# Eight first projections as seven half-size products each, with their weight sums made by GpSimd and VectorE

## The chip, the cores and the metric

The kernel runs on one core of a Trainium2 chip. The metric is the device time of one execution in microseconds (us). Inside the core, TensorE multiplies matrices into eight PSUM banks, VectorE, ScalarE and GpSimd do elementwise work (GpSimd never on a bank), SyncE and GpSimd start transfers. They run their own instruction lists and meet only at semaphores.

## The reference

A two-layer block on 256 latent and 256 context tokens of width 1024, followed by a second two-layer block. The change touches the first layer's input projection of both token sets and what reads it:

```python
def even_layer_mixer(h, hc, w_in, w_out, lb, onorm_g, lam_p, subln_g, lambda_init, rope, need_ctx):
    p = h @ w_in
    pc = hc @ w_in
    ya, yac = hgrn2_mixer(p[..., :5 * A_WIDTH], pc[..., :5 * A_WIDTH], lb, onorm_g)
    yb, ybc = diff_attention_mixer(p[..., 5 * A_WIDTH:], pc[..., 5 * A_WIDTH:], lam_p, subln_g, lambda_init, rope, need_ctx)
    y = jnp.concatenate([ya, yb], axis=-1) @ w_out
...
def split(a):
    q, ff, fb, i, g = jnp.split(a, 5, axis=-1)
    q = heads(jax.nn.silu(q.astype(F32)) * (A_DK ** -0.5))
...
def gates(f_raw, lb_d):
    f = lb_d + (1.0 - lb_d) * jax.nn.sigmoid(f_raw.astype(F32))
    return 1.0 - f, jnp.log(f)
```

`w_in` is 1024 x 4096: eight pieces of 512 columns. Pieces 0 to 4 are q, the two gates, value and output gate of the gated recurrence; 5 to 7 are query, key and value of the differential attention. `h` is the normed input, scaled and shifted by vectors that a further matrix (`ada_w`) makes from a condition. After the two mixers come the output projection and a mixture of experts; nothing there is changed. All is float32.

## The kernel before

**Tiling.** Activations lie with features on the 128 partitions and 512 tokens (latent, then context) along the row: `H[:, k]` is feature tile k of 8. Weights come in chunks of 2 MB (1024 x 512) in the order of the list `CHUNKS` (line 88) into a ring of six slots (`SLOTS`); chunk n goes to slot n % 6. SyncE starts the loads in that order, each once TensorE has closed its last product on chunk n - 6 (`old_chunk_used`, line 1430). `("in1", 0, c)` is piece c of `w_in`, `("ada", l, c)` a modulation chunk.

**Banks.** TensorE's `open_job` takes the next bank of a cycle that `in_banks` sets, or a named one, and waits until the bank's last result was taken; `close_job` tells that it is filled. The readers call `result` (wait until filled) and count the bank as taken. `place_of` and `last_job` hold what stands where.

**Projections.** `project` (line 547) makes four output tiles of a chunk, each from 8 products of 128x128 weights with 512 token columns; `project_tokens` (563) does it with tokens as the output's partitions. One float32 matmul is two instructions in the profile. The order on TensorE is (lines 630 to 757):

1. chunk 5, then 6, each with a modulation chunk (`ada_main`, line 590; 16 instructions of 512 columns) behind each of its four tiles. VectorE turns the modulation sums (`modulation`, 2077), TensorE folds them (`ada_fold`, 607).
2. four products for the rope of q and k (line 641), which VectorE finishes (`rope`, 2112), and chunk 7.
3. the attention loop, 16 units (head, block of 128 queries) and two more rounds to drain it. Iteration i does the scores of unit i, half a tile of chunk 3 or 4 (`value_half`, `gate_half`), the transposes of unit i - 1 and the output of unit i - 2. VectorE finds the maxima (L2133), ScalarE the exponentials (L1704), VectorE scales and subtracts (L2141 to L2144).
4. squares and sums of the head norm (`head_sums`, 526) with chunk 0 in the middle, then chunks 1 and 2.
5. the diagonal scores of the recurrence ("hd", line 730), which wait for `hgrn_inputs`, three modulation chunks of the second layer, and seven levels of doubling in 14 steps (`STEPS`, line 741), with a modulation chunk in each of the first nine.

**Readers of the projections.** ScalarE copies chunks 5, 6, 3 and 4 out of the banks and takes the sigmoid of 0, 1 and 2 straight from them (L1726 to L1731); VectorE copies chunk 7 (L2126), multiplies q by its sigmoid (L2177) and turns the sigmoids into gates (L2183, L2184). Then it makes `A0` from the diagonals and two products over whole pages (L2195, L2197), for which the first level waits. GpSimd has nothing to do from its first three loads until chunk 2 is projected; then it makes one product per step of the levels (L1543), from and to SBUF like VectorE's of the same steps (L2211, L2220).

**Memory.** `pages` are 13 pieces of 2048 columns, reused by every stage; `extra` (3072 columns) holds ScalarE's copies for the levels.

## Time and profile before

| | us |
|---|---|
| three timed runs | 2184.03, 2185.76, 2185.82 (median 2185.76) |
| profiled execution, span from its first to its last instruction | 2180.4 |
| TensorE busy in it | 2032.8 |
| VectorE busy | 686.1 |
| ScalarE busy | 410.1 |
| GpSimd busy | 96.8 |

The profile gives the span of the profiled execution, not its whole time. An engine is busy while it executes; the instructions that only wait or start transfers do not count. The changed part lies between 44 and 346 us.

### The profile page before, as it was taken

The numbers are of one execution on the slowest core, as the hardware profiler recorded it, in microseconds if no ns is written. First come the engines' busy times: TensorE is split into PE (matmuls) and PEld (weight loads), VectorE is DVE, ScalarE is ACT, GpSimd is POOL, SyncE is SP. The second block draws the span as 40 slices with busy tenths as digits, with TensorE's granted clock in tenths as the row PEclk, the third lists the DMA queues.
The fourth block names the chain that finished last, engine by engine and source line by source line (L and its number), as shares of the span: only waits on it lengthen the run. The fifth ranks groups of instructions, "written<-read, shape, count | busy, mean of one in ns | idle before, by whom it ended". The sixth has DMA issues, their size and how long they took to land. (4 is left out here: it accounts for less than half of the span.)

```text
span 2180.4 us, 25566 instructions
## 1 busy us (share of the span) xinstructions
PE 2032.8 (93%) x10076; PEld 1077.9 (49%) x10076; DVE 686.1 (31%) x1583; ACT 410.1 (19%) x872; POOL 96.8 (4%) x92
## 2 busy tenths in 40 slices
PE   5999999896999999999799799999999899998999
PEld 2345546643334334333475533333333766577887
DVE  3034217525110110111547211111111698711411
ACT  2014302212110110111225211111111232421101
POOL 0000004201000000001000100000000000000000
PEclk9999999997999999999899899999999999798999
DMA  9761118412999999999731599999999723233240
GB/s 361 264 234 39 51 65 312 198 43 98 404 417 406 412 419 407 416 406 403 297 116 37 194 416 428 428 410 429 428 429 418 266 97 112 93 122 130 78 155 20
DMA packets 114655, 570.08 MB, mean 261 GB/s; under 512 B 6288, under 2 KB 20880, under 8 KB 89984
## 3 DMA queue, kind: packets, MB, share of 16 engines
q1 hardware_dynamic: 105440, 537.71, 62.0%
q0 software_dynamic: 6688, 25.65, 3.2%
q10 hardware_dynamic: 2432, 5.38, 0.6%
q8 instruction: 69, 1.13, 0.2%
q14 instruction: 26, 0.21, 0.0%
HBM read 560.20 MB, written 8.52 MB: 261 GB/s over the span
## 5 line engine op out<-in xcount | busy, mean ns | idle before, releaser
L556 PE MATMUL banks<-pages,weight_ring 128*128 128x256 f32 (+1 forms) x1984 | 520.5, 423 | 8.5 <-ACT pages L1676 3.2
L556 PEld LDWEIGHTS banks<-pages,weight_ring 128*128 128x128 f32 x1984 | 378.8, 192 | 149.1 <-issue 102.3
L1029 PE MATMUL banks<-weight_ring,pages 128*64 128x512 f32 x964 | 217.3, 597 | 4.3 <-DMA weight_ring<-in_moe_w_gate 1.5
L2004 DVE TENSOR_TENSOR pages<-banks,pages 128x512 f32<-128x512 f32 (+3 forms) x175 | 100.1, 612 | 366.0 <-PE banks L936 177.6
L1775 ACT ACTIVATE pages<-banks 128x512 f32<-128x512 f32 (+1 forms) x147 | 82.5, 572 | 675.8 <-PE banks L966 133.3
L966 PE MATMUL banks<-weight_ring,pages 128*64 128x512 f32 x896 | 198.6, 598 | 7.8 <-issue 3.1
L2004 DVE TENSOR_TENSOR pages<-pages 128x512 f32<-128x512 f32 (+7 forms) x267 | 166.5, 643 | 13.3 <-POOL pages L1543 3.7
L1651 ACT ACTIVATE pages<-banks 128x256 f32<-128x256 f32 (+2 forms) x196 | 81.4, 441 | 460.8 <-PE banks L556 339.2
L2004 DVE TENSOR_TENSOR pages<-pages,banks 128x512 f32<-128x512 f32 (+1 forms) x41 | 28.2, 688 | 401.4 <-PE banks L1029 175.5
L1029 PEld LDWEIGHTS banks<-weight_ring,pages 128*64 128x64 f32 x964 | 67.4, 137 | 147.4 <-issue 133.2
L966 PEld LDWEIGHTS banks<-weight_ring,pages 128*64 128x64 f32 x896 | 63.0, 138 | 135.9 <-issue 130.3
L1139 PE MATMUL banks<-weight_ring,pages 128*64 128x512 f32 x512 | 114.3, 596 | 6.0 <-DVE pages L2498 5.4
L1139 PEld LDWEIGHTS banks<-weight_ring,pages 128*64 128x64 f32 x512 | 35.0, 137 | 74.3 <-issue 61.7
L570 PE MATMUL banks<-weight_ring,pages 128*128 128x512 f32 (+1 forms) x192 | 70.3, 523 | 0.0
L770 PE MATMUL banks<-pages,weight_ring 128*128 128x512 f32 x128 | 57.2, 606 | 3.2 <-DVE pages L2245 3.2
L1006 PE MATMUL banks<-weight_ring,pages 128*128 128x512 f32 x128 | 55.9, 595 | 0.0
L1424 PE MATMUL banks<-weight_ring,pages 128*128 128x256 f32 x256 | 55.4, 379 | 0.0
L1093 PE MATMUL banks<-weight_ring,pages 128*64 128x512 f32 x224 | 51.2, 598 | 3.9 <-issue 3.9
L599 PE MATMUL banks<-weight_ring,small 128*32 128x512 f32 x384 | 47.3, 616 | 7.6 <-DMA weight_ring<-in_ada_w 6.7
L1057 PE MATMUL banks<-weight_ring,pages 128*64 128x512 f32 x224 | 50.1, 596 | 3.6 <-DVE pages L2498 1.9
L570 PEld LDWEIGHTS banks<-weight_ring,pages 128*128 128x128 f32 x192 | 36.1, 190 | 32.7 <-issue 31.1
L1424 PEld LDWEIGHTS banks<-weight_ring,pages 128*128 128x128 f32 x256 | 48.6, 190 | 6.6
(317 smaller groups left out, 1887.8 us busy)
## 6 DMA issues: line engine op xcount, KB each, us to landing
weight_ring<-in_moe_w_down SPq DMA_DIRECT2D x64, 2048.0 KB, 18.3
weight_ring<-in_moe_w_gate SPq DMA_DIRECT2D x62, 2048.0 KB, 17.7
weight_ring<-in_moe_w_up SPq DMA_DIRECT2D x62, 2048.0 KB, 19.4
weight_ring<-in_ada_w SPq DMA_DIRECT2D x24, 2048.0 KB, 16.3
weight_ring<-in_even_w_in SPq DMA_DIRECT2D x18, 2048.0 KB, 19.8
weight_ring<-in_odd_w_in SPq DMA_DIRECT2D x8, 2048.0 KB, 9.0
weight_ring<-in_odd_w_out SPq DMA_DIRECT2D x6, 2048.0 KB, 8.4
weight_ring<-in_odd_w_qkv SPq DMA_DIRECT2D x3, 2048.0 KB, 14.1
```

Source lines behind the costliest of these rows:

```text
L556: last = pe.matmul(b[:, 0:w], s[:, k, m * P:(m + 1) * P], src(k)[:, t0:t0 + w], start=(k == 0), stop=(k == nk - 1))
L570: last = pe.matmul(b[:, 0:n], src(k)[:, t * P:(t + 1) * P], s[:, k, c0:c0 + n], start=(k == 0), stop=(k == nk - 1))
L770: last = pe.matmul(at, s[:, k + 4 - 4 * half, m * P:(m + 1) * P], (yB, g1)[half][:, k], start=(half == 0 and k == 0), stop=(half == 1 and ...
L966: last = pe.matmul(b[n], xg[:, par, 4 * half + k, 0:64], w_[:, k, 512 * n:512 * n + 512], start=(half == 0 and k == 0), stop=(half == 1 an ...
L1006: last = pe.matmul(b, xg[:, par, 4 * half + k], w_[:, k, 512 * n:512 * n + 512], start=(half == 0 and k == 0), stop=(half == 1 and k == 3))
L1029: last = pe.matmul(to, xg[:, par, k, 64 * half:64 * half + 64], rows, start=(half == 0 and k == 0), stop=(half == 1 and k == 3))
L1093: last = pe.matmul(whole[64 * a:64 * a + 64], hidT[:, f, 64 * half:64 * half + 64], w_[:, f, 512 * a:512 * a + 512], start=(half == 0 and ...
L1139: last = pe.matmul(b[64 * a:64 * a + 64], hidT[:, f, 64 * half:64 * half + 64], w_[:, f, 512 * a:512 * a + 512], start=(half == 0 and f == ...
L1424: last = pe.matmul(b[:, 0:256], yp[:, k, t * P:(t + 1) * P], w_[:, k], start=(k == 0), stop=(k == 15))
L1651: act.activation(dst, b[:, 0:w], func).then_inc(taken_sem(job), 1)
L1775: act.activation(dst, banks_mem[:, use(l, job)[0], 0:n], func).then_inc(moe_taken(l, job, 0)[0], 1)
L2004: return dve.tensor_tensor(out_, a, b, op)
```

## The change

Each of the eight chunks is one level of a seven-product scheme for a product of 2 x 2 blocks. The weights of a chunk are cut into four blocks of 512 features x 256 columns, the tokens' side into four of 512 features x 256 tokens. TensorE makes seven products M1 to M7 of 512 x 256 by 512 x 256; four sums of weight blocks, four sums of token blocks and seven additions of results go with them. A product fills one bank and is 16 instructions of 256 columns.

The token sums T1 to T4 are made once by VectorE. The weight sums of chunks 5, 6 and 7 are made by VectorE, in pages; those of 3, 4, 0, 1 and 2 by GpSimd, in slots of the ring: five `("sum", 0, c)` entries stand in `CHUNKS`, for which nothing is loaded, and the chunks behind them move up by one to five places. ScalarE copies M1 out of its bank (`in1_first`); VectorE adds the other six in (`in1_out`), M5 with two instructions. The quarters of q and of the gates get their sigmoid by ScalarE from SBUF afterwards. In the loop, iteration i < 16 has a product: chunk 3 in iterations 0 to 6, chunk 4 in 7 to 13, the first two of chunk 0 in 14 and 15; its other five stand in the head norm. The three modulation chunks of the second layer move from behind the diagonal scores to in front of them. The temporary row of the head norm moves to another page.

```diff
-          + [("in1", 0, c) for c in (7, 3, 4, 0, 1, 2)]
+          + [("in1", 0, 7)]
+          + [(kind, 0, c) for c in (3, 4, 0, 1, 2) for kind in ("in1", "sum")]
...
+    PRODUCTS = {c: ("M1", "M6", "M2", "M7", "M5", "M4", "M3") for c in range(8)}
+    PRODUCTS[5] = ("M1", "M2", "M6", "M7", "M5", "M4", "M3")
+    PAIR = {5: (3, 4), 6: (5, 6), 7: (4, 5), 3: (6, 7), 4: (7, 6), 0: (6, 7), 1: (5, 0), 2: (7, 6)}
+    IN_FIRST = ("M1", "M2", "M5", "M3")
+    SUMMED = (5, 6, 7, 3, 4, 0, 1, 2)
+    IN1_TO = {5: qB, 6: kB, 7: vB, 3: v1, 4: g1, 0: q1, 1: ff, 2: fb}
+    token_side = [extra[:, 1024 * n:1024 * n + 1024].rearrange("p (k t) -> p k t", k=4) for n in range(3)]
+    TSUM = {"T1": token_side[0], "T2": token_side[1], "T3": H[:, 0:4, NX:NTOK], "T4": token_side[2]}
...
+    def sum_parts(w_, to):
+
+        a11, a12 = w_[:, 0:4, 0:NX], w_[:, 4:8, 0:NX]
+        a21, a22 = w_[:, 0:4, NX:512], w_[:, 4:8, NX:512]
+        return ((0, a21, a22, ALU.add), (2, a11, a21, ALU.subtract), (1, to[:, 0], a11, ALU.subtract),
+                (3, a12, to[:, 1], ALU.subtract))
...
+                "M1": (w_[:, low, 0:NX], H[:, low, 0:NX], 0, 0),
+                "M2": (w_[:, high, 0:NX], H[:, high, 0:NX], 0, 0),
+                "M3": (sums[:, 3], H[:, high, NX:NTOK], 4, 0),
+                "M4": (w_[:, high, NX:512], TSUM["T4"], 0, 8),
+                "M5": (sums[:, 0], TSUM["T1"], 1, 1),
+                "M6": (sums[:, 1], TSUM["T2"], 3, 3),
+                "M7": (sums[:, 2], TSUM["T3"], 2, 2)}[product]
...
+            job = in1_job(c, product)
+            b = open_job(job, PAIR[c][0 if product in IN_FIRST else 1])
+            still, moving = (token_side, weight_side) if c in TOKEN_ROWS else (weight_side, token_side)
+            for a in range(2):
+                for k in range(4):
+                    if c == 5 and a == 0 and product in ("M1", "M2"):
+                        pe.wait_ge(sem("norm_h"), 2 * (k + (4 if product == "M2" else 0)) + 1)
+                    last = pe.matmul(b[:, a * NX:(a + 1) * NX], still[:, k, a * P:(a + 1) * P], moving[:, k],
+                                     start=(k == 0), stop=(k == 3))
+            close_job(job, last)
...
-        project("m1", ("in1", 0, 5), h, KT, 4, NTOK, norm="norm_m1", per_k=2, after=ada_beside(4))
-        project("m1", ("in1", 0, 6), h, KT, 4, NTOK, after=ada_beside(8))
+        for c, first in ((5, 4), (6, 8)):
+            for n in range(7):
+                in1_product(c, n)
+                if n < 4:
+                    ada_main(0, first + n)
...
-            if i < 8:
-                value_half(i)
-            elif i < 16:
-                gate_half(i - 8)
+            if i < 16:
+                in1_product((3, 4, 0)[i // 7], i % 7)
...
-        in_banks(*range(8))
-        head_sums("dn", pages(8).rearrange("p (h t) -> p h t", h=4), pages(9, P, 1664),
-                  lambda: project("m1", ("in1", 0, 0), h, KT, 4, NTOK))
+        def rest_of_query():
+            for n in range(2, 7):
+                in1_product(0, n)
+
+        in_banks(*range(5))
+        head_sums("dn", pages(8).rearrange("p (h t) -> p h t", h=4), RS, rest_of_query)
         for c in (1, 2):
-            project("m1", ("in1", 0, c), h, KT, 4, NTOK)
-
+            for n in range(7):
+                in1_product(c, n)
+
+        in_banks(*range(7))
+        for c in range(3):
+            ada_main(1, c)
         pe.wait_ge(sem("diff_done"), 1)
         pe.wait_ge(sem("hgrn_inputs"), 1)
         for c in range(4):
@@ -735,9 +806,6 @@
                     last = pe.matmul(b[:, hd * P:(hd + 1) * P], kk[:, hd, c * P:(c + 1) * P],
                                      q1[:, hd, c * P:(c + 1) * P], start=(n == 0), stop=(n == 1))
             close_job(job, last)
...
-        in_banks(*range(7))
-        for c in range(3):
-            ada_main(1, c)
...
+        for c in BY_POOL:
+            wait_weights(pool, ("in1", 0, c))
+            filled_by_now(last_job[CHUNKS[NUMBER["sum", 0, c] - SLOTS]])
+            w_, to = slot(("in1", 0, c), KT, 512), sums_of(c)
+            for n, (dst, a, b, op) in enumerate(sum_parts(w_, to)):
+                if n >= 2:
+                    pool.wait_ge(sem("pool_sums"), first_sums(c) + (1 if n == 2 else 3))
+                pool.tensor_tensor(to[:, dst], a, b, op).then_inc(sem("pool_sums"), 1)
...
+        def weight_sums(c):
+
+            wait_weights(dve, ("in1", 0, c))
+            if c == 7:
+                result(dve, in1_job(5, "M3"))
+            w_, to = slot(("in1", 0, c), KT, 512), sums_of(c)
+            for n, (dst, a, b, op) in enumerate(sum_parts(w_, to)):
+                if n >= 2:
+                    dve.wait_ge(sem("sums"), first_sums(c) + (1 if n == 2 else 3))
+                tt(to[:, dst], a, b, op).then_inc(sem("sums"), 1)
...
+            if product in ("M6", "M2"):
+                wait_taken(dve, in1_job(c, "M1"))
+                dst, plus = (second if product == "M6" else quad(c, 0, 0)), first
+            elif product == "M7":
+                for done in ("M2", "M6"):
+                    wait_taken(dve, in1_job(c, done))
+                dst, plus = first, second
+            elif product == "M5":
+                wait_taken(dve, in1_job(c, "M7"))
+                tt(quad(c, 1, 1), b, first, ALU.add)
+                dst, plus = second, second
+            elif product == "M4":
+                dst, plus = quad(c, 1, 0), first
+            else:
+                wait_taken(dve, in1_job(c, "M5"))
+                dst, plus = quad(c, 0, 1), second
+            tt(dst, b, plus, ALU.add).then_inc(taken_sem(job), 1)
...
+        dve.wait_ge(sem("norm_h"), 16)
+        low, high = slice(0, 4), slice(4, 8)
+        token_sum("T1", H[:, low, NX:NTOK], H[:, low, 0:NX])
+        token_sum("T3", H[:, high, NX:NTOK], H[:, low, NX:NTOK])
+        dve.wait_ge(sem("sums"), 1)
+        token_sum("T2", H[:, high, NX:NTOK], TSUM["T1"])
+        weight_sums(5)
+        dve.wait_ge(sem("sums"), 3)
+        token_sum("T4", H[:, high, 0:NX], TSUM["T2"])
...
+        for c in (5, 6):
+            for product in PRODUCTS[c][1:5]:
+                in1_out(c, product)
+            weight_sums(c + 1)
+            for product in ("M4", "M3"):
+                in1_out(c, product)
         modulation(1, 0, 4, 8)
...
+        for product in ("M6", "M2", "M7", "M5"):
+            in1_out(7, product)
...
+                c, product = (3, 4, 0)[i // 7], PRODUCTS[0][i % 7]
+                if product != "M1":
+                    in1_out(c, product)
...
+            for product in ("M6", "M2", "M7", "M5"):
+                in1_out(1 + d, product)
+            for product in ("M4", "M3"):
+                in1_out(1 + d, product)
+            for m in (2, 3, 0, 1):
+                dve.wait_ge(sem("in1_sigmoid"), 4 + 4 * d + (3 if m >= 2 else 4))
...
```

## Rows read from the trace of the kernel before

**Rows 1.** The page: TensorE's busy time, and its granted clock in 40 slices (tenths).

```profile
PE 2032.8 (93%) x10076; PEld 1077.9 (49%) x10076; DVE 686.1 (31%) x1583; ACT 410.1 (19%) x872; POOL 96.8 (4%) x92
...
PEclk9999999997999999999899899999999999798999
```

**Rows 2.** Timeline, 40 to 151 us: start, us, engine, line, ..., [idle before, releaser].

```profile
43.07 6.49 ACT L1676 ACTIVATE pages<-pages,small 128x256 f32<-128x256 f32 x16 [2.75 <-DVE pages L2026]
...
44.12 9.72 PE L556 MATMUL banks<-pages,weight_ring 128*128 128x512 f32 x16 [1.60 <-ACT pages L1676]
...
53.77 1.93 PE L599 MATMUL banks<-weight_ring,small 128*32 128x512 f32 x16
...
55.63 7.13 PE L556 MATMUL banks<-pages,weight_ring 128*128 128x512 f32 x16
...
64.54 7.13 PE L556 MATMUL banks<-pages,weight_ring 128*128 128x512 f32 x16
...
119.03 0.33 PE L614 MATMUL banks<-pages,small 128*32 128x32 f32 x16 [0.90 <-DVE pages L2082]
...
122.86 27.63 PE L570 MATMUL banks<-weight_ring,pages 128*128 128x512 f32 x64
```

**Rows 3.** TensorE's timeline from chunks 1 and 2 to the first level.

```profile
274.59 55.17 PE L556 MATMUL banks<-pages,weight_ring 128*128 128x512 f32 x128 [1.85 <-DVE pages L2177]
...
331.70 9.01 PE L735 MATMUL banks<-pages 128*128 128x128 f32 x64 [1.94 <-issue]
...
346.20 2.89 PE L752 MATMUL banks<-pages,extra 128*128 128x128 f32 x16 [0.20 <-DVEq L2200]
```

**Rows 4.** Line 1424: ns min/median/max, first and last start (us), form.

```profile
L1424 PE MATMUL banks<-weight_ring,pages x256: 379/379/379, 2119.7 to 2174.7; 128*128 128x256 f32 x128
```

**Rows 5.** VectorE's timeline: the transposes, and the end of the ropes.

```profile
118.19 0.45 DVE L2081 STREAM_TRANSPOSE pages<-banks 128x256 f32<-128x256 f32 x1 [69.28 <-PE banks L599]
...
128.88 1.42 DVE L2004 TENSOR_TENSOR pages<-pages 128x512 f32<-128x512 f32 x2
```

**Rows 6.** VectorE's timeline in the levels, and GpSimd's products by line.

```profile
352.21 1.23 DVE L2004 TENSOR_TENSOR pages<-pages 128x1024 f32<-128x1024 f32 x1 [2.20 <-POOL pages L1543]
...
358.91 3.66 DVE L2004 TENSOR_TENSOR pages<-pages 128x1024 f32<-128x1024 f32 x1
...
362.49 1.40 DVE L2245 COPY_PREDICATED pages<-pages,banks 128x512 f32<-128x512 uint32 x2
...
L1543 POOL TENSOR_TENSOR pages<-pages x13: 1963/3151/3617, 349.2 to 397.1; 128x1024 f32<-128x1024 f32 x13
```

**Rows 7.** The ring's tile, 70 to 120 us: issue ns, first and last start.

```profile
L1444 SPq DMA_DIRECT2D weight_ring<-in_ada_w x4: 368/1976/5542, 80.6 to 85.1; - x4
...
DMA to landing us min/median/max: 7.9/18.7/21.7
```

**Rows 8.** Windows: last three columns are granted clock, DMA share, GB/s.

```profile
87.00:90.00 3.00, 3.00 (x14) 1.02 (x16) 0.00 (x0) 0.45 (x1) 0.00 (x0) 1.00 1.05 388
...
334.00:336.00 2.00, 2.00 (x11) 2.00 (x11) 0.69 (x1) 2.00 (x2) 0.00 (x0) 0.50 1.04 419
```

**Rows 9.** TensorE's timeline behind waits of 3.5 and 3.2 us.

```profile
29.07 3.51 PE L599 MATMUL banks<-weight_ring,small 128*32 128x512 f32 x16 [3.50 <-DMA weight_ring<-in_ada_w]
...
402.35 3.67 PE L770 MATMUL banks<-pages,weight_ring 128*128 128x512 f32 x8 [3.19 <-DVE pages L2245]
```

**Rows 10.** The loop's timeline: unit 1's probabilities ready, and turned.

```profile
159.70 0.75 DVE L2144 SCALAR_TENSOR_TENSOR pages<-pages 128x512 f32<-128x512 f32 x1
...
164.40 0.60 PE L665 MATMUL banks<-small,pages 128*128 128x128 f32 x4
```

**Rows 11.** VectorE's timeline: a gate, the last diagonal, the whole-page products.

```profile
323.64 0.55 DVE L2183 TENSOR_SCALAR pages<-pages,small 128x512 f32<-128x512 f32 x1 [5.86 <-ACT pages L1651]
...
340.74 0.69 DVE L2004 TENSOR_TENSOR pages<-banks,small 128x512 f32<-128x512 f32 x1 [1.09 <-PE banks L735]
...
341.47 4.62 DVE L2004 TENSOR_TENSOR pages<-pages 128x2048 f32<-128x2048 f32 x2
```

More of the change, by code:

```diff
@@ L215, in landed_value @@
     def landed_value(n):
-        return 16 * sum(1 for m in range(n % SLOTS, n + 1, SLOTS) if CHUNKS[m][0] != "moe")
+        return 16 * sum(1 for m in range(n % SLOTS, n + 1, SLOTS) if CHUNKS[m][0] not in ("moe", "sum"))
     def wait_weights(eng, name):
@@ L1501, in _ @@
         for name in CHUNKS[:MOE0]:
-            if name in last_job:
+            if name in last_job and name[0] != "sum":
                 load(name)
@@ L1690, in _, with in1_first @@
         shift("norm_m1", 0, 0, NTOK)
[L1691 to L1694 removed]
+        def in1_first(c):
+            job = in1_job(c, "M1")
+            act.activation(temps(c)[0], halved(result(act, job)), ACT.Copy).then_inc(taken_sem(job), 1)
+        for c in (5, 6, 7):
+            in1_first(c)
         for i in range(18):
@@ L1724, in _ @@
         wait_taken(act, ("dn", "sum"))
[L1725 to L1733 removed]
+        act.activation(RS, RS, ACT.Sqrt).then_inc(sem("head_root"), 1)
+        QUADS = (("M2", 0, 0), ("M5", 1, 1), ("M4", 1, 0), ("M3", 0, 1))
+        for c in (0, 1, 2):
+            if c:
+                in1_first(c)
+            for product, row, col in QUADS:
+                wait_taken(act, in1_job(c, product))
+                to = quad(c, row, col) if c else q_sig(row, col)
+                act.activation(to, quad(c, row, col), ACT.Sigmoid).then_inc(sem("in1_sigmoid"), 1)
+        for product in ("M4", "M3"):
+            wait_taken(act, in1_job(4, product))
+        for m in range(4):
             act.activation(g1[:, m], g1[:, m], ACT.Silu)
@@ L2125, in _ @@
                 rope(("rope1", half, pair), src[:, 2 * pair:2 * pair + 2, 0:NX], cos1, sin1, rope_tmp, "rope_done")
-        for s in range(4):
-            evac(("m1", ("in1", 0, 7), s), vB[:, s])
+        for product in ("M6", "M2", "M7", "M5"):
+            in1_out(7, product)
+        for product in ("M4", "M3"):
+            in1_out(7, product)
         def diff_negmax(i, m):
```

124 lines of the change are left out of this document (66 added, 58 removed).

## The prediction

> **What bounds the kernel now.** I read the page's first two parts, then TensorE's timeline, then who TensorE waited for. TensorE is busy 2032.8 of 2180.4 us and the granted clock is nine tenths or more in 35 of the page's 40 slices, so nearly always at the full one of its two levels, 2.4 GHz, not 1.2 [rows 1]. So work taken from TensorE shortens the run unless something else arrives too late. The change lies in the first 350 us, and there the timeline has three kinds of stretch: projections in which TensorE waits for nothing [rows 2], a loop of attention units in which its next work is ready before it comes to it, and short joints where it waits for one other engine [rows 2, 3]. Everything behind 346.20 is unchanged and starts when its inputs are there; I carry the shift found there to the end.
>
> The span is 2180.4 us. The page does not give what lies around it; the median of the three timed runs, 2185.76, is 5.4 more. I sum against the span and take the 5.4 as constant.
>
> **TensorE's work.** A chunk is 64 instructions of 512 columns: 27.63 us, 0.43 each [rows 2]. After: 7 products x 4 k x 2 output tiles x 2 instructions = 112 of 256 columns. The trace has this very form, 128x128 weights and 256 columns: 256 of them start from 2119.7 to 2174.7, 55.0/255 = 0.216 us each, weight loads included [rows 4]. So a product is 16 x 0.216 = 3.45, a chunk 24.15, and it saves 3.4. Chunks 5, 6, 7, 1 and 2 save 3.4 each = 17.1. In the attention loop an iteration had 8 instructions of 512 columns (3.45) and gets one product (3.45): no gain there, but the loop now carries 16 products, all of chunks 3 and 4 and two of chunk 0. Of chunk 0 five are left, 17.25 in place of 27.6: 10.3. Total **27.4 gained**.
>
> **Chunks 5 and 6, VectorE's sums.** VectorE has nothing to do there before (it is idle 69 us before 118.19 [rows 5]). The normed input is whole at 43.07 + 6.49 = 49.6 [rows 2]. Then T1, T3, T2 and three weight sums stand before M6, each 1024 elements wide: 1.23 us when GpSimd is quiet [rows 6], 7.4 with gaps, so done at 57.1. TensorE gets to M6 after a slow start (its first 16 instructions take 9.7 where 7.1 is normal [rows 2], and that stays): 44.1 + 2.7 + two products 6.9 + two modulation chunks of 1.85 + switches 0.4 = 57.8. Cost 0, with 0.7 to spare. If it is missed, it costs the difference once.
>
> **The ring.** Chunk 6 has a modulation chunk after each of its first four products. The load of the first waits until chunk 5 is used, and takes 7.9 us to land; that queue was empty, and it started at 80.6 [rows 7]. Before, TensorE asked for it at 53.77 + 4 x 8.91 = 89.4 [rows 2], 0.9 after it landed. Now chunk 5 ends at 53.77 + 3 x 8.91 + 1.9 - 3.4 = about 79.0, it lands at 86.9, and TensorE asks for it at 79.0 + 3.45 + 0.2 = 82.6. **Lost 4.3.** The next three land every 2.1 MB / 388 GB/s = 5.4 [rows 8] and are asked for every 3.45 + 0.2 + 1.85 = 5.5: just in time. A 4.3 us gap can drop the clock: after an idle 3.5 us the next 16 instructions took 3.51 instead of 1.93, after 3.2 us 8 of 512 columns took 3.67, 0.43 apart as ever [rows 9]. I take the fall: 3.5 us at half clock, **lost 1.7** (bounds 0 and 2.7, the slow start of chunk 5).
>
> **The joint before the ropes.** TensorE waits 0.9 for the transposes, which come right behind its last modulation chunk [rows 2, 5]. Now VectorE must first finish chunk 7's four sums (its weights land at about 108.6; four at 1.23 plus chunk 6's M5 end near 116.5) and drain M4 and M3 (0.7 each): a wait of 2.1, **lost 1.2** (0.8 to 2).
>
> **Chunk 7 and GpSimd's first sums.** VectorE runs the ropes (to 130.3 before [rows 5], the same place now, since the joint comes out where it was), then drains M6 of chunk 7, for which TensorE's M7 waits (same bank). M7 is due at 123.0 + 3 x 3.45 = 133.4; VectorE alone would be done at 131.5. But chunk 3's weights land at 117.3 + 7.9 = 125.2, and then GpSimd starts four sums on VectorE's data. Beside GpSimd's products VectorE's operation with two SBUF inputs takes 3.66 instead of 1.23 at worst, while one that reads a bank stays at 0.70, and GpSimd's own takes 2.0 to 3.6, median 3.15 [rows 6]. About 3.3 us of rope work is exposed; doubled, it ends the drain at 135.1: **lost 1.7** (0, if the port is free, to 5, if it is tripled). The sums themselves (4 x 3.15 = 12.6 a chunk) are 20 to 50 us early everywhere: chunk 3 is needed from the second loop iteration, chunks 1 and 2 land when 3 and 4 are used up, and the five take 63 us of an engine whose first product now starts at 349.2 [rows 6].
>
> The Trainium skill ("GPSIMD Engine Reference", section "Key points") says that GpSimd shares its SBUF interfaces with VectorE and contends with instructions that have two SBUF inputs or run in a two-port mode. The trace agrees on the first kind (1.23 against 3.66); no row here shows the second, to which the scaling in the loop could belong. Its side-by-side table gives 4.5 us for a 2048-wide add, so an estimate of 2.25 for one sum; by it GpSimd is done in 9 us and the sum of this forecast stays.
>
> **The loop.** VectorE gets one or two drains (0.69 each, as a bank-reading operation of this width [rows 11]) per iteration of some 5.4. The probabilities were ready at 160.4, TensorE turned them at 164.40 [rows 10]: 3.9 of slack hides the drain (0.7 or 1.4) and some contention. Two softmax operations are wide and have SBUF inputs only, the longer takes 0.75 [rows 10]; doubled they cost 1.5 at most. Cost 0, bounds 0 and 12 (rival C).
>
> **Chunks 0 to 2.** TensorE waited 1.85 for the scaling of q to free a bank [rows 3]; M1 of chunk 1 goes to bank 5, long free. **Gained 1.85**; next late is the drain, 0.7 behind products 3.45 apart.
>
> **The tail.** Before: idle 1.94, score diagonals 9.01, then 5.5 for three modulation chunks: the first level starts at 346.20, 16.5 after the projections [rows 3]. VectorE's A0 and its two 2048-wide products (4.62) were hidden under the modulation chunks [rows 3, 11]. Now these chunks stand in front. They need bank 7, drained 0.85 after M3, then 5.4; the four gate scalings (0.55 and a shorter one behind it, about 1.0 each; with the last sigmoid they end 5.0 after M3 [rows 11]) hide under that. The diagonals take 4 x 1.78 = 7.1 at the full clock (VectorE got the last of them 0.69 + 1.09 behind the third [rows 11]); their 9.01 had a stretch at a granted clock of 0.50 [rows 8]. Then TensorE has nothing until 0.7 + 4.62 + 0.2 later: 5.5. Together 18.9: **lost 2.4** (1.5 to 4.3, if the diagonals stay slow). The gap of 5.5 probably drops the clock at the first level, which GpSimd and VectorE wait for: **lost 2.0** (0 to 4).
>
> **Sum:** 27.4 - 4.3 - 1.7 - 1.2 - 1.7 + 1.85 - 2.4 - 2.0 = 15.9. Span 2164.5; time 2185.8 - 15.9 = **2169.9**.
>
> **Rivals.** A, the forecast, with its own range 2166 to 2174: 0.55.
> B, the gaps leave the clock alone and the ropes are not slowed: 3.7 + 1.7 less lost, 2164.5. For it: a 3.2 us gap without a fall [rows 9]. Against: two gaps are longer. 0.20.
> C, GpSimd slows VectorE's scaling in the loop beyond the slack. Over some 40 us of sums, 7 iterations, VectorE's all-SBUF operations cost 1 us above it each: 7 more, 2177 (2174 to 2181). Against: 3.9 of slack. 0.13.
> D, slower than before: each of the seven all-SBUF operations of a unit, the 128x1 ones too, waits behind a whole GpSimd sum. At 1.4 us each a unit's chain grows by 9.8, 5.9 over the slack, in 7 iterations 41 lost, less 16: 2211; it turns slower than before from 16/7 = 2.3 over the slack, 0.9 us per operation. For it: 3.66 against 1.23 looks like standing behind an instruction. Against: VectorE and GpSimd alternate there without such small waits. 0.04.
> E, nothing gained: a sum is late on every chunk (each M6 waits 3.4), which eats the saving: needs sums over 9 us apiece in place of 3.15; or the drains stall the products. About 2184. 0.08.
>
> A measurement here tells 0.2%, 4.4 us, from no change. Faster by more: A, B, C nearly whole, 0.88; within: 0.06; slower: 0.06. The range leaves out D, E and the ends of C: 2162 to 2178.
>
> **What would show it.** Right: TensorE's products 16 instructions in 3.45; a wait of about 4.3 for a modulation chunk near 83; chunk 7 starting near 123 as before, the loop near 149, chunk 1 some 20 earlier, the first level some 18 earlier, and an idle 5.5 before it; the granted clock at 0.50 after both gaps. Wrong: a wait for GpSimd's sums on TensorE, loop iterations above 5.6, VectorE releasing M7 later than 138, or the shift at the first level not carried to the end.

## The result and the profile after

The change made no gain, and a small loss that is clear of noise: 2188.56 us, median of 20 runs (2185.27 to 2192.57), against 2184.04 for the kernel before on the same chip; ratio 1.0015, 95% interval 1.0008 to 1.0022. Forecast was 2169.9, range 2162 to 2178. The profiled span went from 2180.4 to 2183.4 us; of the 15.9 us forecast none is left, and 3.0 are lost on top: 18.9 us to explain.

The page after, TensorE's busy time and the granted clock [rows 1]:

```profile
PE 2015.0 (92%) x10460; PEld 1153.6 (53%) x10460; DVE 753.1 (34%) x1651; ACT 406.1 (19%) x864; POOL 142.9 (7%) x112
...
PEclk9999999897999999999899899999999999798999
```

TensorE is busy 17.8 us less, and idle 20.8 us more. What runs at half clock counts as busy, so the 17.8 understate the work saved (27.4 by forecast). Line numbers below are the changed kernel's unless said otherwise (710 the seven products, 658 modulation chunks, 820 the levels, 838 the first half of the output projection, 2085 VectorE's two-input operations, 1609 GpSimd's sums).

TensorE's timeline after, from chunk 5 to chunk 7 [rows 2]: start, us, ..., [idle before, releaser].

```profile
71.61 3.62 PE L710 MATMUL banks<-extra,weight_ring 128*128 128x256 f32 x16
75.06 3.62 PE L710 MATMUL banks<-pages 128*128 128x256 f32 x16
78.52 3.62 PE L710 MATMUL banks<-pages,weight_ring 128*128 128x256 f32 x16
...
86.66 3.51 PE L658 MATMUL banks<-weight_ring,small 128*32 128x512 f32 x16 [4.52 <-DMA weight_ring<-in_ada_w]
...
118.71 0.33 PE L673 MATMUL banks<-pages,small 128*32 128x32 f32 x16 [1.47 <-DVE pages L2163]
...
122.50 3.62 PE L710 MATMUL banks<-weight_ring,pages 128*128 128x256 f32 x16
...
135.85 3.69 PE L710 MATMUL banks<-pages 128*128 128x256 f32 x16 [2.82 <-DVE pages L2085]
```

Products start 3.45 apart, the ring costs 4.52 of waiting and 1.6 of half clock (3.51 instead of 1.93), chunk 7 starts at 122.50: as forecast. (The first product starts at 43.26, where the kernel before has 44.12 [rows 2]. Nothing ahead of it was changed; over all traces of this document that start lies between 43.26 and 47.32.) From there on it is worse.

VectorE's timeline after: the rotations of q and k, then the scaling in the loop's first unit (155.15) and in its last (234.01 and 236.20). Behind it, GpSimd's sums:

```profile
123.34 1.42 DVE L2085 TENSOR_TENSOR pages<-pages 128x512 f32<-128x512 f32 x2
...
125.73 3.45 DVE L2085 TENSOR_TENSOR pages<-pages 128x512 f32<-128x512 f32 x2
129.43 0.69 DVE L2085 TENSOR_TENSOR pages<-banks,pages 128x512 f32<-128x512 f32 x1 [0.25 <-DVE pages L2085]
130.15 4.54 DVE L2085 TENSOR_TENSOR pages<-pages 128x512 f32<-128x512 f32 x2
...
155.15 2.60 DVE L2280 SCALAR_TENSOR_TENSOR pages<-pages 128x512 f32<-128x512 f32 x1
...
234.01 2.03 DVE L2278 TENSOR_SCALAR pages<-pages 128x256 f32<-128x256 f32 x1
...
236.20 2.33 DVE L2280 SCALAR_TENSOR_TENSOR pages<-pages 128x256 f32<-128x256 f32 x1
```

```profile
126.02 20.25 POOL L1609 TENSOR_TENSOR weight_ring<-weight_ring 128x1024 f32<-128x1024 f32 x8 [123.03 <-DMA weight_ring<-in_even_w_in]
...
150.05 9.91 POOL L1609 TENSOR_TENSOR weight_ring<-weight_ring 128x1024 f32<-128x1024 f32 x4 [3.79 <-PE banks L710]
...
233.54 9.63 POOL L1609 TENSOR_TENSOR weight_ring<-weight_ring 128x1024 f32<-128x1024 f32 x4 [28.67 <-DMA weight_ring<-in_even_w_in]
```

Each slow operation of VectorE lies inside a GpSimd group: 3.45 and 4.54 for what takes 1.42, 2.60 for 0.75, 2.03 and 2.33 in the last unit for 0.35 and 0.48. The one that reads a bank stays at 0.69.

TensorE's timeline after, the end of the loop, the tail and the first output half [rows 3, 9]:

```profile
238.58 0.44 PE L758 MATMUL banks<-small,pages 128*128 128x128 f32 x2 [1.87 <-DVE pages L2280]
...
241.50 2.12 PE L592 MATMUL banks<-pages,small 128*32 128x128 f32 x32 [1.18 <-ACT pages L1801]
243.55 8.82 PE L710 MATMUL banks<-pages,weight_ring 128*128 128x256 f32 x32
...
320.81 7.41 PE L806 MATMUL banks<-pages 128*128 128x128 f32 x64
333.71 3.79 PE L820 MATMUL banks<-pages,extra 128*128 128x128 f32 x16 [5.49 <-DVEq L2346]
337.42 2.71 PE L658 MATMUL banks<-weight_ring,small 128*32 128x512 f32 x16
...
395.31 6.25 PE L838 MATMUL banks<-pages,weight_ring 128*128 128x512 f32 x8 [6.49 <-DVE pages L2391]
```

The first level is 12.5 us ahead of the kernel before [rows 3]. The windows after say at which clock (last three columns: granted clock, DMA share, GB/s): half, behind the 5.49 and the 6.49 wait.

```profile
334.00:338.00 4.00, 4.00 (x20) 0.50 1.05 386
396.00:400.00 4.00, 4.00 (x6) 0.50 0.00 0
```

The 6.49 wait was in no sum of mine. The first output half is opened on bank 4 by name. With the reset of the bank cycle moved in front of the score diagonals, the levels' cycle starts four banks on, and bank 4 holds the very last level result, drained at 395.2; before, it held an earlier one. TensorE then does 8 instructions in 6.25 where 3.67 were needed [rows 9]. Of the 10.1 us by which VectorE's last level copy is ahead (393.85 against 403.94), 4.5 arrive at the side scores.

The rest goes in a stage that the change does not touch: the experts' first layer, counted here from the start of the router's matmuls to the start of the next projection. It begins 4.4 us ahead of the kernel before and ends 4.4 behind it: the stage takes 580.25 instead of 571.51. ScalarE's timeline at the first expert of that layer, before and then after:

```profile
566.73 0.59 ACT L1823 ACTIVATE pages<-banks 64x512 f32<-64x512 f32 x1
567.50 0.61 ACTq L1825 DMA_DIRECT2D y_rows<-pages  x1
568.17 0.59 ACT L1827 ACTIVATE pages<-banks 64x512 f32<-64x512 f32 x1 [0.84 <-PE banks L1101]
```

```profile
562.60 0.59 ACT L1904 ACTIVATE pages<-banks 64x512 f32<-64x512 f32 x1
563.65 5.00 ACTq L1906 DMA_DIRECT2D y_rows<-pages  x1
568.70 0.59 ACT L1908 ACTIVATE pages<-banks 64x512 f32<-64x512 f32 x1 [5.51 <-issue]
```

The same store (ACTq: ScalarE's sequencer) takes 5.00 us to issue instead of 0.61. VectorE's cast of the next expert's row numbers, GpSimd's fetch and TensorE follow late (a 5.04 wait for the fetched rows at 583.04). "Issue" means that nothing the profile shows held the engine.

### The profile page after: what moved, and what is told of

Read it like the earlier page. It is cut to its first block and busy times, and to the rows that moved or that the text cites. A ratio compares the mean times of both kernels' runs of the same rounds, so it can differ in the third digit from the quotient of the medians.

```text
span 2183.4 us, 26495 instructions
## 1 busy us (share of the span) xinstructions
PE 2015.0 (92%) x10460; PEld 1153.6 (53%) x10460; DVE 753.1 (34%) x1651; ACT 406.1 (19%) x864; POOL 142.9 (7%) x112
## 3 DMA queue, kind: packets, MB, share of 16 engines
q8 instruction: 81, 1.33, 0.2%
## 5 line engine op out<-in xcount | busy, mean ns | idle before, releaser
L615 PE MATMUL banks<-pages,weight_ring 128*128 128x256 f32 (+1 forms) x1664 | 377.2, 388 | 5.1 <-ACT pages L1753 1.6
L2085 DVE TENSOR_TENSOR pages<-banks,pages 128x512 f32<-128x512 f32 (+3 forms) x231 | 137.8, 629 | 468.6 <-PE banks L1004 177.8
L2085 DVE TENSOR_TENSOR pages<-pages 128x512 f32<-128x512 f32 (+11 forms) x268 | 173.9, 668 | 19.5 <-PE banks L852 7.8
L1728 ACT ACTIVATE pages<-banks 128x256 f32<-128x256 f32 (+2 forms) x172 | 67.9, 419 | 343.2 <-PE banks L615 220.2
L710 PE MATMUL banks<-pages,weight_ring 128*128 128x256 f32 x320 | 77.0, 398 | 1.2 <-ACT pages L1753 1.2
L1609 POOL TENSOR_TENSOR weight_ring<-weight_ring 128x1024 f32<-128x1024 f32 x20 | 49.4, 2493 | 190.7 <-DMA weight_ring<-in_even_w_in 186.6
## 6 DMA issues: line engine op xcount, KB each, us to landing
weight_ring<-in_moe_w_down SPq DMA_DIRECT2D x64, 2048.0 KB, 17.8
```

The lines of the kernel that those rows point to most:

```text
L615: last = pe.matmul(b[:, 0:w], s[:, k, m * P:(m + 1) * P], src(k)[:, t0:t0 + w], start=(k == 0), stop=(k == nk - 1))
L710: last = pe.matmul(b[:, a * NX:(a + 1) * NX], still[:, k, a * P:(a + 1) * P], moving[:, k], start=(k == 0), stop=(k == 3))
L1728: act.activation(dst, b[:, 0:w], func).then_inc(taken_sem(job), 1)
L2085: return dve.tensor_tensor(out_, a, b, op)
```

## The experiments

The first two are the two kernels once more, each for a second trace, to tell an accident of one execution from a property of the program. A kernel with one execution (here, and the three that pad the kernel before) is read by its stages alone: the 20 executions of the kernel before spread over 10 us.

> The kernel before, once more, for a second trace of it. Theory S (the experts' stage shifts rigidly, and the changed kernel lost 8.5 us in it by one accident: a store issued by ScalarE that took 5.0 us): the stage from the router's matmuls to the next projection takes 571.5 again, within 1. Rival V (the stage varies from run to run by several us whatever the kernel): another length, by 3 us or more, or a store of several us here too.

> The changed kernel, once more, for a second trace. Theory S: the first 412 us repeat within 0.5 (first level at 333.7); if the 5.0 us store was an accident of one run, the stage takes 572 to 574 in place of 580.3 and the span is 2176. Rival P (it belongs to the program's own phase, since the stores and the loads keep their distance): 580 again, and a store of some 5 us.

Measured: the experts' first layer takes 569.90 in the second trace of the kernel before (0.6 outside the "within 1" of theory S) and 580.05 in that of the changed kernel (580.05 and 580.27 in the next two kernels as well). So rival P holds: the loss belongs to the program, and a stage that starts 2 to 11 us earlier than the kernel before's shows the same. The store takes 4.49 to issue.

Of the 1.6 us between the two traces of the kernel before, 1.5 lie ahead of TensorE's first matmul on fetched rows (526.05 in the first trace), where it was at full clock sooner. From that matmul to the end of the stage they take 541.80 and 541.69, the changed kernel's 550.53 and 550.32: a loss of 8.7, steady to 0.2. This shorter stretch is given below too.

Outside that stage the traces repeat less well. The changed kernel's first level starts at 336.29 instead of within 0.5 of 333.71, all of it lost before the loop. In the kernel before, a half clock comes and goes at two places between its two executions. TensorE's timeline in the second one:

```profile
241.68 28.93 PE L556 MATMUL banks<-pages,weight_ring 128*128 128x512 f32 x64
...
402.18 6.54 PE L770 MATMUL banks<-pages,weight_ring 128*128 128x512 f32 x8 [3.03 <-DVE pages L2245]
```

In its first execution chunk 0 took 27.73, and the first output half 3.67 behind a wait of 3.19 [rows 9]. So single traces show the half clock behind the head sums and at the first output half, not what the change adds to it.

```
# bank cycle
+        in_banks(*range(7))
         for step, (n, g) in enumerate(STEPS):
```

> The changed kernel with the bank cycle started anew in front of the levels, as the kernel before had it. Theory B: the idle 6.5 us before the first half of the output projection falls to about 3.2, the half clock behind it goes, and the cross scores start 5 us earlier (396 in place of 401.4); if the experts' stage carries it, 2183.5, 5 less than the changed kernel. Rival M (the experts' stage is set by its transfers and swallows a shift): the cross scores move, the end does not: 2188.

Measured: 2184.44, ratio 0.9997 (0.9986 to 1.0008), as theory B had it (2183.5). TensorE's timeline in this kernel:

```profile
392.73 3.67 PE L839 MATMUL banks<-pages,weight_ring 128*128 128x512 f32 x8 [3.44 <-DVE pages L2392]
396.24 3.73 PE L853 MATMUL banks<-pages 128*128 128x128 f32 x32
```

The wait is 3.44, near the 3.19 before the change, and full clock follows; first level to side scores takes 62.1 instead of 67.7 us. Of these 5.6, **3.0 us of waiting were the bank's name**. The other 2.6 are half clock, which the kernel before has at this place in one execution and not in the other, so how much of it the name brought is open. The timed runs give 4 back. It stays ahead behind the experts too (1065.16 against 1072.21 there), so rival M falls.

```
# order
-        in_banks(*range(7))
-        for c in range(3):
-            ada_main(1, c)
         pe.wait_ge(sem("diff_done"), 1)
 ...                       (score diagonals)
+        in_banks(*range(7))
+        for c in range(3):
+            ada_main(1, c)
         for step, (n, g) in enumerate(STEPS):
```

> The changed kernel with the three modulation chunks behind the diagonal scores again, and the bank cycle started anew with them, as before. Theory B: the wait of 5.5 us before the first level goes, the diagonals wait about 5 for the gates instead, so the first level starts within 1 us of 333.7, but no half clock slows the levels (2.4 gained), and the banks give 5.6: cross scores at 394, total 2181 if the experts carry it. Rival O (the order alone had cost the 2.4 that I forecast): first level at 331. Rival M: 2188.

Measured: 2184.03, ratio 0.9992 (0.9981 to 1.0003), the same as with the banks alone, and not the 2181 expected. The wait before the first level is gone and the diagonals wait 4.94 instead, as theory B said. But the levels gain less than its 2.4: from the first level to the first output half 57.4 us against 58.6 with the banks alone. The modulation chunks in front of the diagonals bring the first level 1.7 us closer to the head sums (92.3 against 93.9 us) and give these 1.1 back. Their order costs nothing that the timed runs show; what cost was the cycle's reset that moved with them.

What was open: the 10 us in the experts. The changed program has 929 instructions more (26495 against 25566 on the pages): TensorE 804, VectorE 107, GpSimd 25, ScalarE 7 fewer. Empty semaphore increments shift an engine's later instructions; they cost some time of their own where the engine has none to spare, as the last runs show. Theory F says that the loss hangs on the place of an engine's instructions in its program, which comes to it in packets.

```
# 7 on ScalarE (on top of the bank cycle), behind the gate's SiLU
+        for _ in range(7):
+            act.sem_inc(sem("lb_exp"), 1)
```

> The last look left a loss of 9 to 10 us that all four kernels with the seven products show in the experts' first layer (router's matmuls to the next projection 580.1 to 580.3 us, against 569.9 and 571.5 before the change), and it begins with ScalarE's first store to y_rows, whose issue takes 4.4 to 5.0 us instead of 0.6. The changed program has 7 fewer instructions on ScalarE in front of that store (290 instead of 297, waits included). This kernel is the one with the bank cycle set back, plus 7 empty semaphore increments on ScalarE behind the gate's SiLU, nothing else. Theory F (instructions that ScalarE has still to fetch at that store, by their place in its program): the store's issue 0.6 us, the stage 570 to 572 us, the run 9 us under the kernel with the bank cycle alone, about 2175. Rival G (the five added ring entries put the experts' weights in other slots): the stage stays 580, the store's issue 4.4, the time 2184 as before. Rival H (TensorE's, VectorE's or GpSimd's instructions, which are more than before, are what stands elsewhere): as G.

Measured: 2177.4, ratio 0.9963 (0.9950 to 0.9976), and in ScalarE's timeline

```profile
563.41 0.61 ACTq L1909 DMA_DIRECT2D y_rows<-pages  x1
564.07 0.59 ACT L1911 ACTIVATE pages<-banks 64x512 f32<-64x512 f32 x1 [0.84 <-PE banks L1170]
```

The stop is gone, but the stage is 576.9, not 570 to 572: a third of the loss in the trace (the timed ratio fell by more, 0.0034 or 7.4 us). Theory F holds for this store and is not the whole; G and H fall for the store, not yet for the rest.

```
# the kernel before, ScalarE: 249 empty increments
+            for _ in range(8 if i < 16 else 0):          (each attention unit)
+                act.sem_inc(sem("lb_exp"), 1)
 ...
+            for _ in range(9 if step < 9 else 8):        (each step of the levels)
+                act.sem_inc(sem("lb_exp"), 1)
```

> The kernel before with 249 empty semaphore increments on ScalarE, 8 in each of the 16 attention units and 8 or 9 at each of the 14 steps of the levels: its first store to y_rows then stands 249 = 256 - 7 instructions further. The instruction queues' packets are 16 KB each (69 packets, 1.13 MB in the profile before), and if a packet is 256 instructions of one engine (an assumption that this run tests), the store stands as far from the packet's edge as it does in the changed kernel. Theory F with that packet: the store's issue 4.4 to 5 us, the experts' first layer 578 to 581 us instead of 569.9 to 571.5, span about 2187 to 2190. F with another packet length, or rivals G and H: 569.5 to 572. The increments themselves stand where ScalarE waits and may add 0 to 2 us outside the stage.

Measured: span 2189.8, the stage 578.18, and

```profile
570.27 4.68 ACTq L1829 DMA_DIRECT2D y_rows<-pages  x1
575.00 0.59 ACT L1831 ACTIVATE pages<-banks 64x512 f32<-64x512 f32 x1 [5.18 <-issue]
```

A kernel without any of the change now has the stop. 249 = 256 - 7 makes it, 7 unmakes it: the step is 256 instructions of the engine or a part that divides 256, such as 128, which no run here tells apart. The stage is at the lower end of the 578 to 581 expected.

What was left showed in TensorE's timeline of the kernel with 7 increments, as a stop of its own behind the tenth of 32 matmuls of an expert 200 us behind the router, where the kernel before runs all 32 in 7.09:

```profile
694.46 5.31 PE L1035 MATMUL banks<-weight_ring,pages 128*64 128x512 f32 x22 [1.68 <-issue]
```

```
# TensorE: 220 (or, in the kernel before, 36) empty increments in the levels
             if step == 11:
                 ada_fold(2, 12)
+            for _ in range(16 if step < 10 else 15):     (3 if step < 8 else 2)
+                pe.sem_inc(sem("lb_exp"), 1)
```

> The kernel before with 36 empty semaphore increments on TensorE in the levels' steps (804 = 3 x 256 + 36, so its later instructions stand in their packets as the changed kernel's do). Theory F: the stop of 1.5 to 1.7 us at the experts some 200 us behind the router appears and the stage takes 573 to 576 us instead of 569.9 to 571.5; ScalarE's first store stays at 0.6. Rival V or G: 569.5 to 572.

> The kernel before with both paddings, 249 on ScalarE and 36 on TensorE: nothing of the change is in it but the places. Theory F: the experts' first layer takes 580 to 583 us as in the changed kernel (ScalarE's padding alone 578.2, none 569.9 and 571.5), with the store's issue at 4.4 to 5 and TensorE's stop at 1.5 to 1.7. Rival V or G: 577 to 579.

> The changed kernel as it is, with 7 empty increments on ScalarE and 220 on TensorE and no other edit. Theory F: the experts' first layer 570 to 572.5 us instead of 580.1 and 580.3, and the time 8 to 9.5 us less than the changed kernel's, so 2178 to 2181 and a ratio to before of 0.996 to 0.998. Rival V or G: the stage 576 to 578 (ScalarE's part alone), ratio 0.998 to 1.000.

Measured, the experts' first layer in us, and below it the part from the first matmul on fetched rows on:

```
                      padding: none         ScalarE   TensorE   both
kernel before         571.51, 569.90        578.18    574.30    578.63
changed kernel        580.25, 580.05                            570.95
 with banks set back  580.05                576.90

kernel before         541.80, 541.69        548.39    546.38    548.84
changed kernel        550.53, 550.32                            542.72
 with banks set back  550.73                547.18
```

TensorE's padding alone puts its stop into the kernel before, again behind the tenth of the 32 (of the 22 that follow, the window shows 20),

```profile
702.02 4.51 PE L968 MATMUL banks<-weight_ring,pages 128*64 128x512 f32 x20 [1.94 <-issue]
```

and both together take the stops and nearly all of the loss out of the changed kernel (its store issues in 0.62, and TensorE's 32 instructions run without a stop):

```profile
692.62 7.09 PE L1036 MATMUL banks<-weight_ring,pages 128*64 128x512 f32 x32
```

So 7.7 of the 8.7 us are **the place of the instructions**, on two engines; 1.0 stays open. (The whole stage fell by 9.3, but 1.5 of that is the clock at the router, as in the two traces of the kernel before.)

Both paddings in the kernel before give 578.63, under the 580 to 583 expected and inside the rival's 577 to 579. The losses do not add up there: 4.6 for TensorE and 6.6 for ScalarE alone, 7.1 for both. TensorE's 32 instructions take 7.60 in that run, so its stop is 0.5 in place of 1.94. At this one place it is 0.5 to 1.9 long in the nine traces with the placement, and absent (7.09) in the five without. That run alone would decide nothing; TensorE's padding alone and the changed kernel with both decide for F.

The run with both gives 2183.69, ratio 0.9996 (0.9986 to 1.0006), against 1.0015 for the changed kernel: 4 us regained, less than forecast (2178 to 2181). Its levels took 3.1 us more (70.8 from the first level to the side scores, 67.7 before the padding); a new stop on TensorE stands there:

```profile
391.61 2.02 PE L820 MATMUL banks<-pages,extra 128*128 128x128 f32 x16 [2.10 <-issue]
```

Most of the last steps show a wait of 0.5 to 0.7 put to "issue" as well, which the changed kernel does not have: that is the increments themselves, 15 or 16 to a step. What of the 2.10 is a packet's edge is open.

The last question was what GpSimd's sums cost, and whether a version beats both kernels. It starts from the kernel with banks set back and 7 increments.

```
# GpSimd's sums set later
         for c in BY_POOL:
+            if c == 3:
+                pool.wait_ge(sem("rope_done"), 4)
+            if c in (4, 0):
+                filled_by_now(in1_job(*{4: (3, "M7"), 0: (4, "M2")}[c]))
+            if c == 2:
+                pool.wait_ge(sem("diff_done"), 1)
             wait_weights(pool, ("in1", 0, c))
```

> As the kernel with 7 empty ScalarE increments, and GpSimd's weight sums set out of the way of VectorE: those of chunk 3 behind the fourth rotation of q and k, of chunk 4 behind unit 3's product, of chunk 0 behind chunk 4's third product, of chunk 2 behind the head norm of the first attention (about 262 us instead of 233.5). If GpSimd's sums are what slows VectorE (3.45 to 4.54 us for two operations that took 1.42 undisturbed): TensorE's 2.82 wait at chunk 7's fourth product becomes 0 to 1.5, the loop starts 1 to 2.5 us earlier, unit 0's last operation takes 0.75 instead of 2.60, the 1.87 wait at the last unit and the half clock behind it (1.75) go; together 5 to 7 us less than the kernel with the increments. Rival (the sums then come late for chunk 3's second product, or VectorE's longer work has another cause): 0 to 2 us.

Measured: 2176.55, ratio 0.9951 (0.9938 to 0.9965). In VectorE's timeline the rotations are fast again,

```profile
127.72 1.42 DVE L2094 TENSOR_TENSOR pages<-pages 128x512 f32<-128x512 f32 x2
...
130.11 1.42 DVE L2094 TENSOR_TENSOR pages<-pages 128x512 f32<-128x512 f32 x2
```

the wait in chunk 7 is gone, ropes to loop take 27.8 us instead of 30.9 (32.2 in the kernel with 7 increments), loop to head sums 89.5 instead of 91.7 (89.2 before the change). That is 5.3 or more, as expected. But the medians show 0.9 and the ratios 2.6, with intervals that overlap, so time alone does not tell these two kernels apart: chunk 2's sums, put at 262 to 273, now slow VectorE in chunk 1 and TensorE waits there instead,

```profile
274.18 3.69 PE L710 MATMUL banks<-pages,weight_ring 128*128 128x256 f32 x16 [2.60 <-DVE pages L2094]
```

```
# the modulation chunks of chunk 6 one product later
-                if n < 4:
-                    ada_main(0, first + n)
+                if c - 5 <= n < c - 1:
+                    ada_main(0, first + n - (c - 5))
```

> As the kernel with the sums moved, and the four modulation chunks between chunk 6's products set one product later (behind products 2 to 5 instead of 1 to 4). TensorE's 4.5 us wait for the ring at the first of them (3.5 shown as the matmul, 4.52 as the wait) should fall to 0.9 or less, and the half clock behind it (1.7) go: 4.5 to 5.5 us less than the kernel with the sums moved, about 2163 to 2166, below both the kernel before and after. Rival: the wait is one of bandwidth, not of place, and the same time is lost at the next modulation chunk or chunk 7's weights: 0 to 1.5 less.

Measured: 2174.3, ratio 0.9947 (0.9932 to 0.9961), far from the 2163 to 2166 expected and not to be told from the run before. TensorE's waits now:

```profile
88.96 1.93 PE L658 MATMUL banks<-weight_ring,small 128*32 128x512 f32 x16 [1.03 <-DMA weight_ring<-in_ada_w]
...
106.60 1.92 PE L658 MATMUL banks<-weight_ring,small 128*32 128x512 f32 x16 [1.06 <-DMA weight_ring<-in_ada_w]
118.53 0.33 PE L673 MATMUL banks<-pages,small 128*32 128x32 f32 x16 [2.90 <-DVE pages L2172]
```

The 4.4 wait and its half clock are gone, but 1.06 comes back at the last modulation chunk, 1.4 at the fold that waits for it, and the half clock behind that. The rival (0 to 1.5, the wait comes back at the next chunk) holds: the trace keeps 0.8 of the 5 up to the loop. The half clock behind the head sums is back here (8.55 for 7.07), although no sum of GpSimd is near.

The last kernel lets chunk 2's sums start at the head sums and adds TensorE's 220 increments.

```
             if c == 2:
-                pool.wait_ge(sem("diff_done"), 1)
+                filled_by_now(("dn", "sum"))
```

> The kernel with the bank cycle set back, 7 empty ScalarE increments, GpSimd's sums moved and the modulation chunks one product later, with two things more: chunk 2's sums start when the head sums are in (about 240 us) instead of behind the head norm (262), and 220 empty semaphore increments on TensorE in the levels' steps, where it waits for VectorE. What is left of the loss in the experts' first layer shows as a stop of TensorE's own of 1.5 to 1.7 us in front of an expert's matmuls (idle put down to issue, at 692 to 694 us) that the kernel before does not have, and some 2 us more around the first expert. TensorE's program grew by 804 instructions (929 in all, of which VectorE 107, GpSimd 25, ScalarE 7 fewer); 804 + 220 = 4 x 256. Theory F (place of the instructions, 256 to a packet, on TensorE too): the stage 570 to 572.5 us instead of 575.8, no such stop, and the 2.6 us wait in chunk 1's fourth product gone: 5 to 7 less than the last kernel, 2167 to 2169. Rival V (VectorE's 107 further instructions are what stands elsewhere) or G (ring slots): the stage 575 to 577, 2171 to 2173. A cost of the 220 increments themselves would show in the levels (level 1 to the first output half 58.7 us in the last kernel).

Measured: 2172.26, ratio 0.9936 (0.9923 to 0.9950), the lowest and 0.64% under the kernel before. The wait in chunk 1 is gone, and so is TensorE's stop at the expert. But the stage took 574.1 instead of 570 to 572.5, and the levels 2.7 more than without the increments, with the 2.10 stop at the same step as above. The time lies in the 2171 to 2173 of rivals V and G, the stage between their 575 and F's 572.5: something that this document does not name is left in the experts. The kernel cannot be told from the one before it in time (2174.3): the padding gives 1.7 in the experts and takes 2.7 in the levels.

## Why the prediction was wrong

By its own steps, in us of the two first traces; the last column adds to 18.9:

```
step                                 forecast       measured              short by
products, 16 instructions            3.45           3.45                  0
ring wait, half clock                4.3 + 1.7      4.52 + 1.6            0
joint before the ropes               1.2 more       0.6 more              0 (chunk 7 at 122.50)
M7 of chunk 7                        1.7            2.8                   1.1
loop, start to head sums             0              91.7 for 89.2         2.5
half clock behind the head sums      not there      8.82 for 7.07         1.8 (comes and goes)
gap before the first level           5.5            5.49                  0
half clock in the levels             2.0            2.4 with the rest     0.4
first output half's bank             not there      10.1 ahead to 4.5     5.6 (3.0 wait, 2.6 clock)
side scores to the router            0              4.5 ahead to 4.4      0.1
experts, first layer                 0              8.7                   8.8
behind them                          0              1.4 regained         -1.4
```

The zeros of the first three rows hold the 0.86 by which this trace was ahead before the change began. The 1.4 of the last row is inside what the kernel before shows alone: 1112.6 and 1109.8 behind the stage in its two traces.

(The mark "chunk 1 some 20 earlier" was a slip: by the forecast's own terms it was 13.6, and 20.4 at the end of chunk 2; measured 8.5 and 15.0.)

**Right:** the saving, its size, VectorE's sums, the ring, the order of the tail. **Failed:** the step "Everything behind 346.20 is unchanged ... I carry the shift found there to the end", and with it 13 of the 18.9. Two things behind 346.20 did change with the edit, though no line there did: the number of the bank that a result falls into, and the place in each engine's program. The first could have been counted from the code; nothing in the trace of before announced the second.

**Mis-sized:** the cost of GpSimd beside VectorE, some 5.0 (2.8 in chunk 7, 2.2 at the loop's last unit) where 1.7 stood. The price of one operation was within what [rows 6] bound (3.66 for 1.23 there, 4.54 for two that take 1.42 here, so 3.2 times instead of 3), but the rope term took "doubled" where these rows said three times. What failed in the loop is "3.9 of slack hides ...". That slack was read at unit 1 [rows 10]. At the last unit of the kernel before, VectorE's scaling and TensorE's transpose behind it are only 1.5 apart:

```profile
234.80 0.48 DVE L2144 SCALAR_TENSOR_TENSOR pages<-pages 128x256 f32<-128x256 f32 x1
```

```profile
236.81 0.38 PE L665 MATMUL banks<-small,pages 128*128 128x128 f32 x2
```

There GpSimd's group at 233.54 adds 3.5 to two operations, and TensorE waits 1.87. The group at 150.05 adds 2.3 at unit 0, and costs nothing: the slack there is 3.6, and TensorE's first units start 4.71 and 5.15 apart, as before (4.69 and 5.13). In the kernel with the sums moved, the sums of three chunks stand in the middle of the loop and cost nothing that shows: from unit 0 to unit 15 it takes 81.41, the changed kernel 81.42, the kernel before 81.12, so 0.3 of the loop's 2.5 is not GpSimd's. Rival C named the mechanism and looked for it in seven units of the loop; it was in one.

That kernel shows the 2.8 and the last unit's 2.2 gone. The 1.8 of half clock behind the head sums is gone there too, but it is not shown to be GpSimd's: the second trace of the kernel before has 1.2 of it, and the last two kernels 1.5, without a sum in the loop's last unit.

GpSimd also slowed a form that the trace of before had not shown beside it: the 128x256 TENSOR_SCALAR with one SBUF input and no bank, 2.03 at 234.01 where the kernel before has 0.35. By the Trainium skill ("GPSIMD Engine Reference", section "Key points") the contention meets instructions with two SBUF inputs and those in a two-port mode; the forecast said that no row showed the second kind. This one fits it, though no row tells the mode.

**Left open:** the half clocks that come and go, 1.0 us of the experts, the share of VectorE's and GpSimd's shifted instructions there, and some 0.4 us of the levels.

## What to carry to other kernels

Saved work counts only as far as it is followed: before carrying a gain past the edit, count again every cycle that the edit shifts (banks, ring slots), and look at what is opened by a fixed number. Slack read in the middle of a pipelined loop need not hold in its last unit (1.5 us here for 3.9); read it unit by unit, and put a contending helper's work into the middle. Take a second trace of both kernels before putting down a half clock to the change. When an untouched stage grows by the same amount in every run, compare the waits named "issue" engine by engine, and shift one engine's program by a few empty instructions before believing a data cause.

## What the runs showed of the hardware

An engine can stop for some us at a place that its instruction count sets. On ScalarE the store's issue took 4.43 to 5.00 in six traces with one placement and 0.61 or 0.62 in the eight others; 7 and 256 - 7 instructions change one into the other. On TensorE 36 more instructions (804 = 3 x 256 + 36) bring a stop of 0.5 to 1.9, behind the same matmul in all seven traces whose rows show where, and 220 more (to 4 x 256) take it away.

The instruction queue's row on the page has 69 packets with 1.13 MB before and 81 with 1.33 MB after, 16 KB each. Their number follows TensorE's placement and not the length of the program: 36 increments on TensorE raise it from 69 to 78, 220 lower it from 81 to 73, 249 or 7 on ScalarE leave it. So some packets must be fetched more than once in one placement; no run here shows which. The Trainium skill ("Runtime: NRT & Kernel Launch", section "Instruction fetch mechanics") gives blocks of 16 KiB, 256 instructions, and calls the cost of crossing one mostly hidden. The packets' size agrees and the shifts fit it; the cost does not here.

Where the stop fell, the DMA engines were full with the experts' weights, in the changed kernel's window

```profile
562.00:569.00 7.00, 7.00 (x42) 1.00 1.01 427
```

The kernel before has 1.01 in the same window, and no stop. That the fetch is slow because the transfers are full was not tried by itself; that it is a fetch at all is the reading that fits the shifts, as the profile only says "issue".
